# The remainders of 20 weight units in each layer's attention steps made by GpSimd instead of VectorE

## The reference

```
h = rms(x) * (1 + sc1) + sh1
u = h @ w_in                  # 4096 gate columns, then the columns of four token mixers
out_a = pool_mixer(xa)        # multi-scale pooling
out_b = diff_attention(...)   # 4 heads, two softmaxes per head: softmax(q1 k1) - lam * softmax(q2 k2)
out_c = fourier(xc)
out_d = softmax_attention(...)# MLA, 4 heads, one softmax per head
proj   = einsum('btnw,nwd->btnd', branches, w_branch)
merged = sum(sigmoid(gates) * proj)
x = x + g1 * (merged @ w_out)
h2 = rms(x) * (1 + sc2) + sh2
x = x + g2 * conv_ffn(h2)     # w_up, depthwise convolution of width 3, gated, w_down
```

## Time and profile before

| what | value |
|---|---|
| median of three runs | 1223.99 us |
| the profiled execution, its own time | 1223.51 us |
| its span | 1221.7 us |
| PE busy | 1208.0 us (99%) |
| DVE busy | 901.4 us (74%) |
| ACT busy | 575.6 us (47%) |
| POOL busy | 136.8 us (11%) |
| granted TensorE clock | full in the whole span |
| remainders on DVE (L980) | 251 of 1272 ns on average |

### The profile page before, as it was taken

One profiled execution on the slowest core, in us unless ns is written; L12 is line 12 of the kernel. 1 busy time (PEld: TensorE's weight loads), 2 busy tenths in 40 slices (PEclk: granted clock), 3 DMA queues, 4 the chain that ended last, 5 costly groups with the idle time before them and its releaser, 6 DMA issues.

```text
span 1221.7 us, 19781 instructions
## 1 busy us (share of the span) xinstructions
PE 1208.0 (99%) x7816; PEld 1149.7 (94%) x7816; DVE 901.4 (74%) x1671; ACT 575.6 (47%) x949; POOL 136.8 (11%) x109
## 2 busy tenths in 40 slices
PE   8999999999999999999999999999999999999998
PEld 7987999989989999999989889999998999999998
DVE  5597877748689999986876965765686887887432
ACT  3445564643365544532354455645425554454321
POOL 0232000008300000000202500000271000000000
PEclk9999999999999999999999999999999999999999
DMA  9763433444744444469664522332345334334443
GB/s 370 291 220 125 147 117 112 172 139 161 253 173 144 167 156 159 169 216 322 214 234 163 189 87 87 104 104 87 104 167 196 122 124 135 122 123 136 134 142 121
DMA packets 53532, 198.82 MB, mean 163 GB/s; under 512 B 6784, under 2 KB 7200, under 8 KB 51904
## 3 DMA queue, kind: packets, MB, share of 16 engines
q1 hardware_dynamic: 53120, 196.86, 46.0%
q0 software_dynamic: 320, 0.69, 0.2%
HBM read 195.25 MB, written 2.27 MB: 162 GB/s over the span
## 4 chain that ended last, share of the span: by engine, by line
PE 93%; DVE 2%; POOL 2%; DMA 1%; issue 1%; ACT 0%; SPq 0%; DVEq 0%; POOLq 0%; ACTq 0%
PE bank L1444 27%; PE bank L1446 27%; PE bank L1445 26%; PE bank L1743 1%; PE bank L1723 1%; PE bank L1512 1%; DVE w_lo L980 1%; DMA start_ada<-start_ada 1%; PE bank L1517 1%; PE bank L1516 1%; POOL wide L653 1%; PE bank L1713 1%; POOL merge_sum L655 1%; PE bank L1501 1%; PE bank L1698 1%
## 5 line engine op out<-in xcount | busy, mean ns | idle before, releaser
L1444 PE MATMUL bank<-act_hi,w_hi 128*128 128x384 f32 x1368 | 465.0, 340 | 0.7 <-DVE act_lo L1055 0.3
L1446 PE MATMUL bank<-act_hi,w_lo 128*128 128x384 f32 x1368 | 457.8, 335 | 0.0
L1445 PE MATMUL bank<-act_lo,w_hi 128*128 128x384 f32 x1336 | 446.6, 334 | 0.0
L980 DVE TENSOR_TENSOR w_lo<-w_raw,w_hi 128x1024 fp32r<-128x1024 f32 x251 | 318.9, 1272 | 114.6 <-ACT w_hi L662 113.6
L662 ACT ACTIVATE w_hi<-w_raw 128x1024 fp32r<-128x1024 f32 x251 | 264.3, 1054 | 167.8 <-DMA w_raw<-stream 167.7
L1444 PEld LDWEIGHTS bank<-act_hi,w_hi 128*128 128x128 f32 x1368 | 257.1, 188 | 10.7 <-issue 6.5
L1446 PEld LDWEIGHTS bank<-act_hi,w_lo 128*128 128x128 f32 x1368 | 256.8, 188 | 0.0
L1445 PEld LDWEIGHTS bank<-act_lo,w_hi 128*128 128x128 f32 x1336 | 251.0, 188 | 0.6
L1446 PE MATMUL bank<-mlp_hi,w_lo 128*128 128x384 f32 x352 | 118.3, 336 | 0.0
L1444 PE MATMUL bank<-mlp_hi,w_hi 128*128 128x384 f32 x352 | 118.3, 336 | 0.0
L1445 PE MATMUL bank<-mlp_lo,w_hi 128*128 128x384 f32 x352 | 118.3, 336 | 0.0
(11 more groups left out here) (246 smaller groups left out, 1576.0 us busy)
## 6 DMA issues: line engine op xcount, KB each, us to landing
w_raw<-stream SPq DMA_DIRECT2D x251, 512.0 KB, 3.3
ada<-ada_rows SPq DMA_DIRECT2D x48, 512.0 KB, 4.4
start_ada<-start_ada SPq DMA_DIRECT2D x8, 1024.0 KB, 17.9
ada_norm<-ada_w SPq DMA_DIRECT2D x16, 512.0 KB, 5.8
ada<-ada_w SPq DMA_DIRECT2D x8, 512.0 KB, 5.5
start_raw<-start_w SPq DMA_DIRECT2D x8, 448.0 KB, 18.5
ada_head_a<-ada_w SPq DMA_DIRECT2D x5, 512.0 KB, 7.3
cond_spread_mix<-cond_rows SPq DMA_DIRECT2D x2, 1024.0 KB, 7.9
```

Of the source, the lines that this page charges most:

```text
L980: V.tensor_tensor(wlo[s][:, :], raw[s][:, :], whi[s][:, :].bitcast(F32), ALU.subtract).then_inc(lo_ready, 1)
L1444: T.matmul(out, wb[s][0][:, w, :], hi[k], start=first and k == 0, stop=False)
L1445: T.matmul(out, wb[s][0][:, w, :], lo[k], start=False, stop=False)
L1446: ins = T.matmul(out, wb[s][1][:, w, :], hi[k], start=False, stop=last and k == n - 1)
```

## The change

In each layer GpSimd makes the remainders of the units that steps 2 to 21 split, 20 of 24, with the same subtraction of the same tiles. Before the first it waits until VectorE has made the one before (step 1's), and before each until ScalarE has made that unit's `w_hi`. VectorE leaves these 20 out, and before step 22's remainder it waits until GpSimd's last one is made, so that `lo_ready` still counts the units in order.

```
+POOL_STEPS = range(2, 22)
...
+                for i in POOL_STEPS:
+                    n = l * UNITS + G0 + PREP_GATES + i + 2 - SKIP
+                    if i == POOL_STEPS[0]:
+                        pool.wait_ge(lo_ready, n)
+                    pool.wait_ge(hi_ready, n + 1)
+                    nc.gpsimd.tensor_tensor(wlo[n % SLOTS][:, :], raw[n % SLOTS][:, :], whi[n % SLOTS][:, :].bitcast(F32), ALU.subtract
+                                            ).then_inc(lo_ready, 1)
...
-                    split(G0 + PREP_GATES + i + 2)
+                    if i == POOL_STEPS[-1] + 1:
+                        dve.wait_ge(lo_ready, l * UNITS + G0 + PREP_GATES + i + 2 - SKIP)
+                    if i not in POOL_STEPS:
+                        split(G0 + PREP_GATES + i + 2)
```

## The result

The changed kernel took 1226.28 us (median of 17 runs, 1225.19 to 1226.68), the kernel before beside it 1224.22 us (median of 17). The ratio is 1.0017, with a 95% interval of 1.0010 to 1.0025: slower by 2.1 us, clear of no change, and a little under the 0.2% that I had set as the bound of "same". The forecast was +2.7 us.

What follows compares the result with a forecast made beforehand. TensorE, busy for 1208.0 of 1221.7 us, was taken as the bound. 0 (removed) + 0 (second layer, differential steps) + 2.65 gave about +2.7 us on 1223.99, so 1226.7 us; range 1223.9 to 1230.5, the forecast's own 1225.3 to 1228.2.

Steps and rivals of the forecast that it cites:

- TensorE is the bound and the relief is worth 0: Attention steps: 40 remainders leaving VectorE, some 46 us, all lie beside TensorE's work, so they save 0.
- GpSimd's remainder takes 2.39 us: A 128x1024 subtraction on GpSimd, extended from rows of 384 and 768 columns: 2.39 us, bounds 1.94 and 2.88.
- the dearer rival: Remainders of 2.9 us or more, by fp32r output or the slowest row as rule: 1229.5 to 1232 us; chance 0.15.
- The engines exclude each other, instruction by instruction: Attention steps: VectorE operations with two SBUF inputs wait out GpSimd's whole instruction, and the reverse; maxima reading PSUM go on.
- The rival in which GpSimd gives way: GpSimd always loses to VectorE in collisions, so nothing is late: 1224.0 us; chance 0.18.
- Nobody waits for GpSimd's remainder: Only TensorE needs the remainder, two steps and some 11 us later, so its longer duration costs 0.
- Differential steps and second layer: Idle time before VectorE's maxima takes up the at most 1.25 us a step of extra load: price 0.
- Steps 13 to 15: First layer: row products and rotation collide with GpSimd, so step 16's maxima come at 223.7 instead of 220.33, 3.4 us late.
- The slack: First layer: step 17's exponentials end 0.75 us before step 18's scores start, so TensorE loses 3.4 - 0.75 = 2.65 us.
- The forecast's own mechanism: GpSimd takes its turn; 1.3 to 4.2 us are lost in the first layer, none in the second; chance 0.63.

Runs made afterwards that it cites:

- run 1: GpSimd makes the remainders of steps 2 to 21 in the second layer only; 1223.74 us against 1224.02 for the kernel before, ratio 1.0000.
- run 2: GpSimd makes the remainders of steps 2 to 11 and 18 to 21 in both layers; 1224.51 us against 1224.02 for the kernel before.
- run 4: The changed kernel with each remainder made in two GpSimd instructions of 512 columns; 1226.24 us against 1224.02 for the kernel before, ratio 1.0017.
- run 7: GpSimd makes one remainder, step 15's in the first layer; 1224.17 us against 1223.85 for the kernel before, ratio 1.0005.

## Why the prediction came out right

- **TensorE is the bound and the relief is worth 0.** Right. Runs 1 and 2 have 20 and 28 remainders off VectorE and are no faster.
- **GpSimd's remainder takes 2.39 us.** Right. Over all 40 the shortest is 2.37 us, in the view of the tile, and the median 2.44, waits included. The rows had given 1.94, 2.39 and 2.88 us; that the middle one fits was a judgement, not a derivation. With fp32r output it takes what rows with fp32 output had given, so the dearer rival fell with both of its open points. The Trainium skill's figure (GPSIMD Engine Reference, elementwise cycle accounting), from which I had estimated 2.25 us, is 5% under the shortest one here.
- **The engines exclude each other, instruction by instruction.** Right, and shown in each timeline above. I had named operations with two inputs; the 2.19 and 2.50 us of a TENSOR_SCALAR with one input from SBUF (0.29 us otherwise) show that it holds for that one as well. The rival in which GpSimd gives way fell: in the pairs of row products GpSimd got its turn each time, in steps 16 and 17 too, where the second product of the pair lasted 3.30 us (226.28 and 232.95). The maxima read PSUM and go on, as I had it; in the change none of them meets GpSimd, but in run 4 one does, in GpSimd's second half (to 229.82), and keeps its 0.55 us:

```profile
228.59 0.55 DVE L1250 TENSOR_REDUCE small<-bank 128x1 f32<-128x384 f32 x1
...
225.67 4.15 POOL L656 TENSOR_TENSOR w_lo<-w_raw,w_hi 128x512 fp32r<-128x512 f32 x2 [6.28 <-ACT w_hi L674]
```

- **Nobody waits for GpSimd's remainder.** Right: no wait of TensorE names it.
- **Differential steps and second layer: 0.** Right, by run 1 and by the unchanged 116.66 us of run 2, whose ten differential steps 2 to 11 have their remainders on GpSimd.
- **Steps 13 to 15.** The mechanism is right, the size of one term was off. In the time of before, the maxima of step 14 came at 209.44 + 0.18 = 209.6 (I had 209.7), the rotation's last product ended at 215.9 (I had 216.1), and the maxima of step 16 came at 223.2 (I had 223.7): 2.85 us late instead of 3.4. The step that was mis-sized is step 15, where I charged GpSimd's whole 2.39 us to VectorE. Measured, the row product lost 3.28 - 1.23 = 2.05 us, 0.34 less, since GpSimd's turn began while the rotation's last product was ending. The same in run 7, 1.90 us. The other 0.2 us of my excess came in before it. A collision costs the wait of the one operation that meets it, here 1.86 to 2.19 us, some 0.2 to 0.5 us less than the other engine's instruction. With the waits as measured the sum closes: VectorE is 0.15 us late as step 13's row products begin (204.83 + 0.18 against 204.86 with 0.46 us idle before it; step 12's rotation product had lasted 2.63 us), then 2.19 - 1.14, 1.86 - 1.14 and 2.05 - 1.14 are added, together 2.8 us.
- **The slack.** 0.75 us by my rows, 0.70 measured five times over: between the end of the exponentials and the scores 0.06 us remain (231.12 to 231.18), which I had counted as slack. The path is the one that I had named. 2.85 - 0.70 = 2.15, and the time says 2.1.
- **Chances.** The forecast's own mechanism happened, in the lower half of its range; +0.17% is within 0.2%, which had 0.41 against 0.55 for slower. So on which side of 0.2% it would fall I had called wrongly, by the 0.55 us that step 15 and the steps before it were put too high.

Neither the change nor a part of it beats the kernel before, and run 2 only gets back to it. There is nothing in these stretches to win, because TensorE doesn't wait in them.

## What to carry to other kernels

Moving elementwise work from VectorE to GpSimd was hardly a relief here, where both read SBUF: in a collision VectorE lost 1.9 to 2.2 us to a 2.4 us instruction in order to save 1.2 us of its own. It was free only where VectorE had idle time, so look for the step without any, not at the mean: here 4 of 40 places carried the whole loss, at a place where VectorE's queue had been full without harm. Find the first thing behind that place that the bound engine waits for, and how long it had been early (0.7 us here); that number decides between nothing and a loss.

## What was not expected of the hardware

- An operation of VectorE with one SBUF input and a per-partition scalar, 128x128 in 0.29 us, waited for GpSimd as the two-input ones do (2.19 and 2.50 us).
- The wait does not depend on the size of what waits: a product of 64 columns took 2.42 us instead of 0.23.
- Waiting for the other engine's turn is shown as busy time of the instruction. VectorE's busy sum fell by 2.3 us where 40 instructions of 1.2 us had been taken away.
